# Attention loop of a streaming encoder: inverse ahead of the maximum, keys' and queries' split in the first step of ten, evictions behind remainders, GpSimd's work a step later

## What is computed

```
each layer:
  x += 1/2 * SwiGLU(RMSNorm(x))                       # FFN 1
  P  = RMSNorm(x) @ w_in -> q|k|v|q_idx|k_idx|w_idx|B|C|xin|gates
  index scores -> top-k keys of every query (128 of 512, 68 of 272)
  A  = softmax(q.k over the chosen keys) @ v           # 8 heads of 64
  Bc = B * conv3_causal(C * xin)                       # 4 blocks of 128 channels
  x += (sigmoid(gA) * (A @ wA) + sigmoid(gB) * (Bc @ wB)) @ w_out
  x += 1/2 * SwiGLU(RMSNorm(x))                       # FFN 2
```

## Time and profile before

| | us |
|---|---|
| median of 3 runs | 2761.95 (2761.6 to 2761.99) |
| the profiled execution's own time | 2763.02 |
| its span in the profile | 2761.2 |
| TensorE busy in the span | 2718.5 (98%) |
| VectorE busy | 1724.7 (62%) |
| ScalarE busy | 1118.1 (40%) |
| GpSimd busy | 1003.5 (36%) |
| mean granted TensorE clock | 0.995 of full speed |

### The profile page before, as it was taken

How to read it: one execution, slowest core, us unless ns; L and a number is a source line. 1 busy time by engine, 2 the same in 40 slices (tenths; PEclk the granted TensorE clock), 3 DMA queues, 4 the chain that set the end, 5 groups by cost and what they waited for, 6 DMA issues and landing times. The chain is left out here.

```text
span 2761.2 us, 46980 instructions
## 1 busy us (share of the span) xinstructions
PE 2718.5 (98%) x18808; PEld 2652.3 (96%) x18808; DVE 1724.7 (62%) x2805; ACT 1118.1 (40%) x1864; POOL 1003.5 (36%) x610
## 2 busy tenths in 40 slices
PE   9999999999999999999999999999999999999997
PEld 8999999997899999999999999998879999999997
DVE  8747576786433693838685747668763347837475
ACT  5424244536432342424443333454464233524242
POOL 2333333345433333333333333333544333333332
PEclk9999999999999999999999999999999999999999
DMA  3222222233122212222222222222331221222222
GB/s 118 92 76 92 77 87 92 87 123 116 62 71 89 76 69 84 85 89 80 92 77 85 75 94 84 79 85 88 131 106 62 76 91 61 84 75 87 92 77 84
DMA packets 72565, 238.04 MB, mean 86 GB/s; under 512 B 8272, under 2 KB 16720, under 8 KB 71888
## 3 DMA queue, kind: packets, MB, share of 16 engines
q1 hardware_dynamic: 57888, 208.30, 21.7%
q10 hardware_dynamic: 14512, 27.51, 2.8%
HBM read 227.52 MB, written 8.27 MB: 85 GB/s over the span
## 5 line engine op out<-in xcount | busy, mean ns | idle before, releaser
L487 POOL TENSOR_TENSOR w_lo<-w_raw,w_hi 128x1024 fp32r<-128x1024 f32 (+1 forms) x254 | 600.7, 2367 | 979.5 <-ACT w_hi L1098 964.2
L1098 ACT ACTIVATE w_hi<-w_raw 128x1024 fp32r<-128x1024 f32 x238 | 252.3, 1060 | 763.4 <-PE lin L615 625.4
L615 PE MATMUL lin<-h_hi,w_hi 128*128 128x320 f32 x1600 | 374.9, 316 | 3.3 <-POOL w_lo L487 2.3
L615 PE MATMUL lin<-h_lo,w_hi 128*128 128x320 f32 x1600 | 365.6, 310 | 0.0
L615 PE MATMUL lin<-h_hi,w_lo 128*128 128x320 f32 x1600 | 365.6, 310 | 0.0
L615 PE MATMUL lin<-g_lo,w_hi 128*128 128x320 f32 x1408 | 320.8, 309 | 0.0
L615 PE MATMUL lin<-g_hi,w_hi 128*128 128x320 f32 x1408 | 320.8, 309 | 0.0
L615 PE MATMUL lin<-g_hi,w_lo 128*128 128x320 f32 x1408 | 320.7, 309 | 0.0
L539 POOL TENSOR_TENSOR lo_A<-raw_even,hi_A 128x512 fp32r<-128x512 f32 x120 | 169.4, 1412 | 373.2 <-ACT hi_A L1143 373.2
L615 PEld LDWEIGHTS lin<-h_hi,w_hi 128*128 128x128 f32 x1600 | 266.1, 189 | 17.1 <-issue 11.9
L615 PEld LDWEIGHTS lin<-h_hi,w_lo 128*128 128x128 f32 x1600 | 268.6, 188 | 0.0
(11 more groups left out here) (330 smaller groups left out, 6252.5 us busy)
## 6 DMA issues: line engine op xcount, KB each, us to landing
w_raw<-wts SPq DMA_DIRECT2D x240, 512.0 KB, 3.5
raw_even<-wts SPq DMA_DIRECT2D x88, 512.0 KB, 4.4
raw_odd<-wts SPq DMA_DIRECT2D x64, 512.0 KB, 4.3
caches<-kcache_in ACTq DMA_DIRECT2D x16, 512.0 KB, 4.0
caches<-vcache_in ACTq DMA_DIRECT2D x16, 512.0 KB, 4.8
x<-x_in SPq DMA_DIRECT2D x8, 320.0 KB, 6.6
k_out<-kT ACTq DMA_DIRECT2D x2, 1280.0 KB, 4.6
v_out<-v_sb ACTq DMA_DIRECT2D x2, 1280.0 KB, 8.6
```

The source lines that it names most:

```text
L487: ins = nc.gpsimd.tensor_tensor(w_lo[:, s, cols], w_raw[:, s, cols], w_hi[:, s, cols].bitcast(F), ALU.subtract)
L615: ins = nc.tensor.matmul(out[:, half, :], w, a[:, half * HALF:(half + 1) * HALF], start=first and n == 0, stop=last and n == 2)
L1098: nc.scalar.activation(w_hi[:, s, :], w_raw[:, s, :], ACT.Copy).then_inc(hi_ready.sem, 1)
```

## The change

On ScalarE, `split_kq` moves from steps 3, 13, 23 (behind the exponential) to the head of steps 0, 10, 20. On VectorE, `invert` of unit u-1 moves ahead of `row_max` of unit u; `lo_kq` moves from steps 4, 14, 24 to steps 0, 10, 20, right behind `row_max`; `pT_lo` then comes ahead of `conv_result`. On GpSimd, `gate_conv` and `weigh_past` for the early tiles move from steps 5 and 6 to 6 and 7; for late tiles 0 to 3 the halves of `low` move from ago 1, 2 to ago 2, 3 (2, 4 for tile 2) and the parts of `convolve` from ago 3, 4 to 5, 6; `gate_conv` and `weigh_past` of the late tiles stay at 3 and 4, and tiles 4 and 5 are dealt as before.

```diff
+LATE_DEAL = {_t: ((2, 4 if _t == 2 else 3), (5, 6), 3) if _t < 4 else ((1, 2), (3, 4), 3) for _t in range(LATE_CONV)}
@@ GpSimd, in the loop over steps, behind normalise(L, step - 1)
-                    if step == 5:
+                    if step == 6:
                         gate_conv(L, 1)
-                    if step == 6:
+                    if step == 7:
                         weigh_past(L, 2)
-                    for ago in range(1, 6):
+                    for ago in range(1, 7):
                         if step - ago not in LATE_DONE:
                             continue
-                        tile = EARLY_CONV + LATE_DONE[step - ago]
+                        late = LATE_DONE[step - ago]
+                        tile = EARLY_CONV + late
                         ct, what = divmod(tile, 3)
-                        if ago < 3:
-                            low(L, CONV_AT + tile + 2, half=ago - 1)
-                        elif ago < 5 and what == 1:
-                            convolve(L, ct, part_=ago - 3)
-                        elif ago == 3 and what == 2:
+                        lows, parts, gated = LATE_DEAL[late]
+                        if ago in lows:
+                            low(L, CONV_AT + tile + 2, half=lows.index(ago))
+                        if what == 1 and ago in parts:
+                            convolve(L, ct, part_=parts.index(ago))
+                        if what == 2 and ago == gated:
                             gate_conv(L, ct)
-                        elif ago == 4 and what == 2 and ct + 1 < CB:
+                        if what == 2 and ago == gated + 1 and ct + 1 < CB:
                             weigh_past(L, ct + 1)
@@ ScalarE
                 for step in range(NU + 4):
+                    if step % 10 == 0 and step // 10 + 1 < PAIRS:
+                        split_kq(L, step // 10 + 1)
...
                         exps(L, step)
                         if kind == "stream" and b + 1 < STREAMS:
                             place_q(L, b + 1)
-                        if step % 10 == 3 and step // 10 + 1 < PAIRS:
-                            split_kq(L, step // 10 + 1)
@@ VectorE
+                    if 0 <= step - 1 < NU:
+                        invert(L, step - 1)
                     if step < NU:
                         row_max(L, step)
                     if step == 0:
                         lo_v(L, 0)
-                    if 0 <= step - 1 < NU:
-                        invert(L, step - 1)
+                    if step % 10 == 0 and step // 10 + 1 < PAIRS:
+                        lo_kq(L, step // 10 + 1)
+                    if 0 <= step - 2 < NU and ATT_UNITS[step - 2][0] == "prompt":
+                        pT_lo(L, step - 2)
                     for tile in done:
                         conv_result(CONV_AT + tile, CONV_RES + tile, 0)
-                    if 0 <= step - 2 < NU and ATT_UNITS[step - 2][0] == "prompt":
-                        pT_lo(L, step - 2)
-                    if step % 10 == 4 and step // 10 + 1 < PAIRS:
-                        lo_kq(L, step // 10 + 1)
```

## The result

The changed kernel takes 2770.0 us in the median (2769.26 to 2772.98, 8 executions) beside 2761.58 (2761.14 to 2762.3, 8 executions) for the kernel before on the same chip: a ratio of 1.0032, with a 95% interval of 1.0023 to 1.0041. The change makes the kernel slower, by 8.4 us. The profiled execution after has a span of 2768.7 and an own time of 2770.49.

A forecast was written before the change was run, and what follows sets the result against it. The prediction took TensorE, busy 2718.5 of 2761.2 us, as the bound. It summed 7.3 us added less 3.63 removed to +3.7 a loop, +7.4 on the 2761.95 median: 2769.4, with an 8-in-10 range of 2762 to 2774.

The forecast's parts named there:

- split in step 0: Start of the loop: split and `lo_kq` delay the maxima, so the logits of units 3 and 4 wait; cost 2.2 us.
- stall of old step 6: TensorE's idle before the logits at 628.21, behind `lo_kq` of old step 4, goes; gain 0.76 us.
- step 10: The split and `lo_kq` delay unit 9's remainder, so `weigh` starts later; cost 1.45 us, from 1.0 to 1.8.
- step 16: Turn of unit 14 gains 0.7 us; the eviction, waiting for a 512-wide remainder, gives back 0.7.
- step 20: Same chain as step 10, without the convolution's remainder but with port meetings with GpSimd; cost 1.25 us, from 0.9 to 2.4.
- eviction, step 24: First piece of a new tile waits for `conv_result`, now behind unit 21's remainder; cost 0.6 us, 0.4 to 0.8.
- logits of step 26, turn of unit 24: Idle behind `lo_kq` of old step 24 and behind a half of `low` goes; gains 0.5 and 0.6 us.
- gate's product in step 26: `gate_conv` starts before the strips' copy and holds VectorE; `weigh` of step 27 loses 0.7 us, 0 to 1.0.
- convolution's remainder, logits of step 36: A half of `low` in step 34 runs under this remainder; unit 35's maximum is late, TensorE loses 0.4 us.
- (a): Rival: port meetings avoided and start-up chains at lower bounds; +0.8 us a loop, 2763.5 us; chance 0.24.
- (b): Rival: the split in steps 0, 10 and 20 is covered, so faster; 2757.3 to 2759.5 us; chance 0.12.
- (c): Rival: each subtraction of step 20 waits out a GpSimd instruction, other meetings last longest; 5.35 us a loop, 2772.7; chance 0.14.

The follow-up runs named there:

- after_filler: Changed kernel with two unused 512-column products added on TensorE in step 2: 2769.51 us against 2762.66 for the kernel before.
- after_first_old: Changed kernel with only pair 1's split back in step 3 and its remainders in step 4: 2766.77 us against 2762.66 for the kernel before.
- after_split38: Changed kernel with `split_kq` at the head of steps 3, 13, 23 and `lo_kq` in 8, 18, 28: 2761.34 us against 2762.66 for the kernel before.
- after: The changed kernel itself, first measurement and profile: 2770.0 us against 2761.58 for the kernel before.
- after_again: The changed kernel itself, measured and profiled a second time: 2769.66 us against 2762.23 for the kernel before.
- after_gate30: The step-30 experiment: changed kernel with `gate_conv` of late tile 2 in step 30, not 26: 2769.41 us against 2762.23 for the kernel before.
- the last version: Kernel before with split in steps 3/13/23, `lo_kq` in 8/18/28, inverse first after step 3, some GpSimd work later, evictions as before: 2755.71 us against 2762.23.

## Why the prediction was right

The predicted time was 2769.4 and the measured 2770.0; slower by over 0.2% had the greatest chance, and it is what came. But the nearness of the sum is in part chance: some of its terms were too large, and one was missing. The steps, each as a distance between the same TensorE instructions in the first loop, after less before:

| step of the prediction | predicted | measured |
|---|---|---|
| split in step 0, up to the logits of step 3 | +2.2 | +2.18 |
| stall of old step 6 gone | -0.76 | -0.77 |
| step 10, up to `weigh` of step 12 | +1.45 | +1.30 |
| step 16: turn of unit 14 gains, eviction loses | -0.7+0.7 | -0.01 |
| turn of unit 18 | -0.7 | -0.70 |
| step 20, up to `weigh` of step 22 | +1.25 | +0.98 |
| eviction, step 24 | +0.6 | +0.59 |
| logits of step 26, turn of unit 24 | -0.5-0.6 | -0.51-0.62 |
| gate's product in step 26, `weigh` of step 27 | +0.7 | +0.48 |
| convolution's remainder, logits of step 36 | +0.4 | +0.39 |
| turn of unit 38 and `weigh` | -0.37 | -0.37 |
| sum, a loop | +3.7 | +2.9 |

**What was right** is the place and the direction of every row. Steps 0, 10 and 20, read before as chains of VectorE's work, came as such. Three details did not: the prediction names `weigh` of steps 12 and 22 as the place of the idle (over 1 us), and most of it stands one instruction earlier, at the turn that waits for the strips (0.92 and 0.65, with 0.29 at `weigh`); the logits of step 3 idle for 0.65 and not 1 to 2; and the row of step 16 nets to nothing out of two terms that were each 0.3 too small, -1.0 and +1.0, because an idle of 0.18 at the logits of step 16 was not counted. **What was mis-sized** are the terms of steps 10, 20 and 26, together 0.64 a loop too high. In step 10 `lo_kq` began at 641.06, which is the 640.8 of the prediction on a trace that is 0.23 later there; but from it to unit 9's remainder (644.48) it took 3.42 and not 3.6 to 3.7. In step 20 the subtractions came as predicted: from the first start to the last end 2.17 us, where the prediction has 2.2 (664.0 to 666.2). What was too long is the rest, from there to the start of `weigh`: 2.3 us (667.77 to 670.05) and not 2.6, of which 0.2 is the strips' copy, held up less by the taps of step 21, and 0.1 the remainder. In the subtractions the two engines ran alternately:

```profile
665.09 2.14 POOL L528 TENSOR_TENSOR tmp<-tmp,tap 128x511 f32<-128x511 f32 x2
665.60 1.33 DVE L2035 TENSOR_TENSOR k_lo<-kT,k_hi 128x512 fp32r<-128x512 f32 x1 [0.94 <-ACT q_hi L1351]
...
666.84 0.93 DVE L2037 TENSOR_TENSOR q_lo<-qT,q_hi 128x512 fp32r<-128x512 f32 x1
```

`k_lo` took 1.33 where it takes 0.70 alone (641.06), and `q_lo` 0.93 where it takes 0.68; the pair of taps took 2.14 where it took 1.68 before. So each waits for the rest of one instruction of the other, and not for a whole pair: +0.9 for VectorE and +0.5 for GpSimd. The step-30 experiment shows the same by a removal: the copy falls from 1.21 to 0.15. The Trainium skill states it as an exclusive lock, in which whichever starts first fully blocks the other (SBUF — State Buffer, "SBUF: two separate sides"); by that rule the trace agrees, and it blocks in both directions; the loss on GpSimd's side is in no term of my sum.

**What was missing** is a term for TensorE's clock. The prediction has two loops of 3.7, and none for the 1.2 GHz level. Measured are two of 2.9, which is 5.8, and the medians of +8.4 and +7.4 leave 2.6 and 1.6, mostly for the clock. That it comes from the long stall of steps 2 and 3 is shown by three runs: with the stall filled (after_filler), shortened (after_first_old) or gone (after_split38), no loop of their profiles shows a half-clock stretch, while four of the six loops of the three profiles that keep the stall in the changed kernel's order (after, after_again, after_gate30) do. The 1.6 too much in the order of the work and the 2 missing for the clock nearly cancel: that the sum came within 0.6 us is luck. No row that I had chosen has such a stretch, but the trace of before has three outside the loops, so the term could have been foreseen.

**The rivals.** (a), smaller additions, would need the chains of steps 0 and 10 at their lower bounds; step 0 came at its full value. (b), the split covered, is excluded by 1.66 and 0.92 us of TensorE idle at the strips and by after_split38, which shows the gain that this rival wrongly expected, but only once the split is moved out of those steps. (c), the lock in full, is excluded by its price and not by its mechanism: each subtraction of step 20 did meet a tap, but waited only for what was left of it (0.63 and 0.25), and `weigh` of step 27 lost 0.5 and not 1.0.

One thing remains open. Why the clock falls in one loop and not in the other after the same idle no run here tells. The Trainium skill (TensorE: Matmul & The Clock Gate, Part 1 on the clock gate) says that the gate's watching runs free of the kernel, so the same program may meet it at different points; the scatter of the executions agrees, and no run here shows it.

## What to carry to other kernels

Before moving work to "an earlier, quieter step", look who is just starting there: at the beginning of a pipeline, and at each point where a new group refills it, the engines wait for each other, and even a microsecond on an engine that is busy for 40% of the span is paid for: here 2.2, 1.3 and 1.0 us in steps 0, 10 and 20 for 1.1 on ScalarE and 1.3 on VectorE. The same split costs 3.6 us a loop more in the first step of ten than in the third and eighth (123.50 against 119.86). Time each part alone and in combination, and lay their traces beside each other, for two parts may remove the same idle time: a change of four parts hid a gain of 2.2 us behind a loss of 7.5, and the parts put where the traces show cover, without the new order of evictions, made 6.5 us of gain.

## What the runs showed of the hardware

A stall of TensorE can cost more than its length. After 2.3 us of idle within 4 us (busy 1.69 of 4.00) the granted clock fell in five of eight loops to 0.50, the 1.2 GHz level, for 3.4 or 6.8 us, which cost 1.5 or 2.9 us more; in others it stayed at 1.00, with the same instructions. The time scatters with it: 3.7 and 4.9 us between executions of the changed kernel, 1.3 for the last version. With two 512-column products, computed for nobody, in the idle time, the clock stayed up in both loops of the profiled run.

A copy of 16 columns in SBUF takes 0.15 us alone and 1.21 when it meets a 640-column product on GpSimd. The profile shows such waiting as busy time of the instruction and not as idle time, on either engine. VectorE's remainder of a transposed tile, read from PSUM, is not lengthened: 0.55 at 667.70 in the changed kernel, beside the taps of 667.19 to 669.07, and 0.56 without them:

```profile
667.19 1.88 POOL L528 TENSOR_TENSOR tmp<-tmp 128x510 f32<-128x510 f32 x2
667.70 0.55 DVE L2028 TENSOR_TENSOR pT<-bank,pT 128x384 fp32r<-128x384 f32 x1
```
